# Keeping half of the attention output in SBUF, and another order of the output projection's loads and sums

## The reference

```
mixed = sigmoid(gate_a) * a + sigmoid(gate_h) * r
h  = h + rms_norm(mixed @ w_o, g_mix_post)
hn = rms_norm(h, g_ffn_pre)
ff = (silu(hn @ w_gate) * (hn @ w_up)) @ w_down
h  = h + rms_norm(ff, g_ffn_post)      # meta tokens dropped
```

## Time and profile before

| | |
|---|---|
| median of 3 runs | 2333.02 us (2331.67 to 2337.22) |
| profiled execution, its time | 2335.76 us |
| profiled execution, its span | 2334.0 us |
| mean granted PE clock over the span | 0.98 |
| busy: PE, DVE, ACT, POOL | 2205.8, 1065.7, 917.3, 461.0 us |
| span of the output projection's first matmul to the first FFN tile | 1465.90 to 1580.15 us |

### The profile page before, as it was taken

How to read it: one execution, slowest core, us unless ns; L and a number is a source line. 1 busy time by engine, 2 the same in 40 slices (tenths; PEclk the granted TensorE clock), 3 DMA queues, 4 the chain that set the end, 5 groups by cost and what they waited for, 6 DMA issues and landing times. The chain is left out here.

```text
span 2334.0 us, 32080 instructions
## 1 busy us (share of the span) xinstructions
PE 2205.8 (95%) x11716; PEld 1845.5 (79%) x11716; DVE 1065.7 (46%) x1727; ACT 917.3 (39%) x1454; POOL 461.0 (20%) x213
## 2 busy tenths in 40 slices
PE   5999999999999999889999998789999999999996
PEld 4988888888888888677777776667888788878785
DVE  5003665665764754366666665373533001421102
ACT  4213354354354453544444443444343223222222
POOL 3110000000000000111111111114444444444443
PEclk8999999999999999999999999899999999999998
DMA  3211112111111111211111110542333233343233
GB/s 142 75 63 64 33 60 64 40 59 63 40 59 56 40 57 40 107 41 46 46 45 45 45 45 28 193 145 89 94 132 98 92 108 108 116 136 99 90 104 122
DMA packets 78714, 182.61 MB, mean 78 GB/s; under 512 B 6864, under 2 KB 27664, under 8 KB 78128
## 3 DMA queue, kind: packets, MB, share of 16 engines
q1 hardware_dynamic: 78640, 181.61, 23.9%
HBM read 152.09 MB, written 29.49 MB: 78 GB/s over the span
## 5 line engine op out<-in xcount | busy, mean ns | idle before, releaser
L1798 POOL TENSOR_TENSOR w_lo<-w_raw,w_hi 128x1024 fp32r<-128x1024 f32 x136 | 331.1, 2435 | 398.9 <-ACT w_hi L1807 398.9
L83 PE MATMUL h_bank<-hn_hi,w_hi 128*128 128x512 f32 (+2 forms) x952 | 374.1, 393 | 3.9 <-PEq L165 2.5
L84 PE MATMUL h_bank<-hn_lo,w_hi 128*128 128x512 f32 (+2 forms) x952 | 356.8, 375 | 0.0
L85 PE MATMUL h_bank<-hn_hi,w_lo 128*128 128x512 f32 (+2 forms) x952 | 356.3, 374 | 0.0
L83 PE MATMUL f_bank<-ffn_in_hi,w_hi 128*128 128x512 f32 x768 | 303.5, 395 | 16.7 <-DVE ffn_in_lo L1987 10.9
L85 PE MATMUL f_bank<-ffn_in_hi,w_lo 128*128 128x512 f32 x768 | 301.8, 393 | 0.0
L84 PE MATMUL f_bank<-ffn_in_lo,w_hi 128*128 128x512 f32 x768 | 301.8, 393 | 0.0
L83 PEld LDWEIGHTS h_bank<-hn_hi,w_hi 128*128 128x128 f32 x952 | 179.6, 189 | 36.7 <-issue 9.9
L85 PEld LDWEIGHTS h_bank<-hn_hi,w_lo 128*128 128x128 f32 x952 | 179.4, 188 | 29.8
L84 PEld LDWEIGHTS h_bank<-hn_lo,w_hi 128*128 128x128 f32 x952 | 179.6, 189 | 28.1 <-issue 3.8
L1807 ACT CAST w_hi<-w_raw 128x1024 fp32r<-128x1024 f32 x136 | 142.5, 1048 | 130.7 <-PE f_bank L85 127.9
(11 more groups left out here) (330 smaller groups left out, 4360.5 us busy)
## 6 DMA issues: line engine op xcount, KB each, us to landing
w_raw<-in_w_ffn SPq DMA_DIRECT2D x136, 512.0 KB, 3.6
w_raw<-in_w_hgrn SPq DMA_DIRECT2D x54, 512.0 KB, 3.6
w_raw<-in_w_out SPq DMA_DIRECT2D x15, 512.0 KB, 4.0
w_raw<-in_w_head SPq DMA_DIRECT2D x9, 512.0 KB, 5.7
X<-in_x SPq DMA_DIRECT2D x8, 520.0 KB, 6.5
values<-v_stage SPq DMA_DIRECT2D x32, 128.0 KB, 1.7
values_h<-values SPq DMA_DIRECT2D x8, 512.0 KB, 4.9
gate_out<-raw SPq DMA_DIRECT2D x8, 512.0 KB, 2.9
```

The lines of the kernel that those rows point to most:

```text
L83: pe.matmul(out, wh, xh, start=start, stop=False)
L84: pe.matmul(out, wh, xl, start=False, stop=False)
L85: return pe.matmul(out, wl, xh, start=False, stop=stop)
L1798: pool.tensor_tensor(w_lo[i][:], w_raw[i][:], w_hi[i][:].bitcast(F32), ALU.subtract).then_inc(w_lo_done, 1)
```

## The change

- Attention: the first half of `mixed` is written to `mixed_first`, an SBUF buffer with a place for each head; only the second half goes to DRAM, from one buffer, `mixed_second`. In the last head, after each step j of both segments, ACT casts (`split_high`) and DVE subtracts (`split_low`) one head's first half, eight in all. Their results lie where the latents lay.
- SP no longer waits for the stores at the end of the block; it waits for them in the next one, ahead of the loads of the second half.
- Output projection: the first half needs no loads. Weight loads 1 and 2 go first, then two loads of four second halves each with weight loads 3 and 4 between. They are split after blocks 2 and 4 (`mixed_hi`, `mixed_lo`). The load of x now stands ahead of weight load 6 and waits for all eight.
- `h_inverse_rms(0)` follows block 12 instead of 11, `add_up_h(0)` stands behind k = 6 of block 12 instead of k = 0; the weight casts and normalizing casts of blocks 13 to 15 have another order on ACT, weight subtractions 14 and 15 another on DVE. The first FFN tile waits for each normalized k-tile by itself; `add_up_o(1)` follows it, and all later stages come one tile later. POOL subtracts weight block 16 before it adds the last square.
- `y_sum` gets a buffer of its own, and some buffers lie elsewhere.

```diff
+        self.mixed_first = sb("mixed_first", [P, KT, HALF])
+        with ExitStack() as place:
+            self.mixed_parts = {x: place.enter_context(t.nc.sbuf_tensor(f"mixed_first_{x}", [P, KT, HALF], F32R))
+                                for x in ("hi", "lo")}
...
-        mixed = [sb(f"mixed{i}", [P, HALF]) for i in range(2)]
+
+        def mixed(h, i):
+            return mixed_second[:].unsqueeze(1) if i else lat.mixed_first[:, bass.ds(h.index(), 1), :]
...
-        mixed_out = [signal(f"mixed_out{i}", 16) for i in range(2)]
+        mixed_out = signal("mixed_out", 16)
+        first_hi, first_lo = t.sem("mixed_first_hi"), t.sem("mixed_first_lo")
...
                         sp.dma_start(w_raw[:], dram_block(t.d["w_head"], p.index() + 1)).then_inc(w_in.sem, 16)
                     if h is not None:
-                        for i in range(2):
-                            mix_done.wait(sp, h, i + 1)
-                            sp.dma_start(dram_head(t.d_mixed, hh)[:, i * HALF:(i + 1) * HALF],
-                                         mixed[i][:]).then_inc(mixed_out[i].sem, 16)
+                        mix_done.wait(sp, h, 2)
+                        sp.dma_start(dram_head(t.d_mixed, hh), mixed_second[:]).then_inc(mixed_out.sem, 16)
 
                 iterations(sp, both)
-                for i in range(2):
-                    sp.wait_ge(mixed_out[i].sem, 16 * HEADS)
...
                             gated.wait(pool, x, i + 1)
                             gate_in[i].wait(pool, x, 32)
-                            pool.tensor_tensor(mixed[i][:], mixed[i][:], rec[i][:], ALU.add
+                            pool.tensor_tensor(mixed(x, i), mixed(x, i), rec[i][:].unsqueeze(1), ALU.add
                                                ).then_inc(mix_done.sem, 1)
...
 
+                def split_high(k):
+                    if k == 0:
+                        piece_done.wait(act, At(HEADS - 1), NP_)
+                    mix_done.wait(act, At(k), 1)
+                    act.copy(lat.mixed_parts["hi"][:, k, :], lat.mixed_first[:, k, :]).then_inc(first_hi, 1)
...
                                 values(p)
                             else:
                                 weights(p, 2)
+                        if last:
+                            split_high(which * QS + j)
...
 
+                def split_low(k):
+                    dve.wait_ge(first_hi, k + 1)
+                    dve.tensor_tensor(lat.mixed_parts["lo"][:, k, :], lat.mixed_first[:, k, :],
+                                      lat.mixed_parts["hi"][:, k, :].bitcast(F32), ALU.subtract).then_inc(first_lo, 1)
...
                         if cur is not None and 2 * j + 3 < TILES:
                             low(cur, 2 * j + 3)
+                        if last:
+                            split_low(which * QS + j)
                     if cur is not None:
                         h, i = cur
                         pv_done.wait(dve, h, (i + 1) * TILES)
                         gate_in[i].wait(dve, h, 32)
-                        mixed_out[i].wait(dve, h, 16, lag=1)
-                        dve.tensor_tensor(mixed[i][:], o_bank[:], gate[i][:], ALU.mult).then_inc(gated.sem, 1)
+                        if i:
+                            mixed_out.wait(dve, h, 16, lag=1)
+                        dve.tensor_tensor(mixed(h, i), o_bank[:].unsqueeze(1), gate[i][:].unsqueeze(1), ALU.mult
+                                          ).then_inc(gated.sem, 1)
...
-            ("unused", [P, FT - 2 * KT - 5, HALF], F32), ("normed", [P, 2, HALF], F32), ("f_rs2", [P, HALF], F32))
+            ("out_sum", [P, FT - 2 * KT - 5, HALF], F32), ("normed", [P, 2, HALF], F32), ("f_rs2", [P, HALF], F32))
...
-        mixed = [acts[1], {"hi": mixed_hi2, "lo": mixed_lo2}]
+        mixed = [mixed_first, {"hi": mixed_hi2, "lo": mixed_lo2}]
...
 
-                for i, (half, first, n) in enumerate(MIXED_LOADS):
-                    src = t.d_mixed[first:first + n, :, half * HALF:(half + 1) * HALF].rearrange("k p n -> p k n")
-                    sp.dma_start(mixed_raw[half][:, first:first + n, :], src).then_inc(m_in[i], 16)
-                    if i < 2:
-                        load_out(i + 1)
-                sp.wait_ge(m_hi, 2 * KT)
-                sp.wait_ge(m_lo, 2 * KT)
-                sp.dma_start(x_res, t.d["x"][:, :, 0:HALF]).then_inc(x_in, 16)
-                for b in range(3, OUT_BLOCKS):
+                load_out(1)
+                load_out(2)
+                sp.wait_ge(mixed_out, 16 * HEADS)
+                for i in range(2):
+                    src = t.d_mixed[i * MP_:(i + 1) * MP_].rearrange("k p n -> p k n")
+                    sp.dma_start(mixed_raw[:, i * MP_:(i + 1) * MP_, :], src).then_inc(m_in[i], 16)
+                    load_out(i + 3)
+                for b in range(5, OUT_BLOCKS):
+                    if b == 6:
+                        sp.wait_ge(m_lo, KT)
+                        sp.dma_start(x_res, t.d["x"][:, :, 0:HALF]).then_inc(x_in, 16)
                     if b == OUT_BLOCKS - 2:
...
+                def weight_lo(count, i):
+                    pool.wait_ge(w_hi_done, count)
+                    pool.tensor_tensor(w_lo[i][:], w_raw[i][:], w_hi[i][:].bitcast(F32),
+                                       ALU.subtract).then_inc(w_lo_done, 1)
+
+                for e in range(OUT_BLOCKS - 1):
                     add_square(e)
                 pool.wait_ge(w_lo_done, OUT_BLOCKS - 1)
-                with pool.Fori(0, FFN_BLOCKS) as j:
+                weight_lo(OUT_BLOCKS, 0)
+                add_square(OUT_BLOCKS - 1)
+                weight_lo(OUT_BLOCKS + 1, 1)
+                with pool.Fori(0, FFN_BLOCKS - 1) as j:
                     for i in range(2):
-                        pool.wait_ge(w_hi_done, 2 * j + (OUT_BLOCKS + i))
-                        pool.tensor_tensor(w_lo[i][:], w_raw[i][:], w_hi[i][:].bitcast(F32),
-                                           ALU.subtract).then_inc(w_lo_done, 1)
...
-                def mixed_hi(q):
-                    half, k = q // KT, q % KT
-                    for i, (of_half, first, n) in enumerate(MIXED_LOADS):
-                        if of_half == half and first <= k < first + n:
-                            act.wait_ge(m_in[i], 16)
-                    act.copy(mixed[half]["hi"][:, k, :], mixed_raw[half][:, k, :]).then_inc(m_hi, 1)
+                def mixed_hi(k):
+                    act.wait_ge(m_in[k // MP_], 16)
+                    act.copy(mixed_hi2[:, k, :], mixed_raw[:, k, :]).then_inc(m_hi, 1)
...
 
                 act.preload_act_table_set("natural_log_exp_and_others")
-                for q in range(3):
-                    mixed_hi(q)
                 weight_hi_out(1)
-                for q in range(3, 2 * KT):
-                    mixed_hi(q)
 
                 beside = {0: [lambda m=m: square_h(m) for m in (0, 1)],
                           1: [lambda m=m: square_h(m) for m in (2, 3, 4, 5)],
-                          2: [lambda m=m: square_h(m) for m in (6, 7)], 3: [lambda: h_inverse_rms(0)],
-                          4: [lambda m=m: normed_hi(m) for m in (0, 1, 2)],
-                          5: [lambda m=m: normed_hi(m) for m in (3, 4, 5)],
-                          6: [lambda m=m: normed_hi(m) for m in (6, 7)]}
-                for b in range(OUT_BLOCKS):
-                    if 2 <= b + 1 < OUT_BLOCKS:
+                          2: [lambda m=m: square_h(m) for m in (6, 7)], 4: [lambda: h_inverse_rms(0)]}
+                for b in range(KT + 5):
+                    if b:
                         weight_hi_out(b + 1)
-                    elif b + 1 == OUT_BLOCKS:
-                        act.wait_ge(o_done, b)
-                        weight_hi(2, At(0), 0, 0)
                     if b == KT:
                         o_inverse_rms(0)
                     projected(b)
+                    if b in (2, 4):
+                        for k in range(MP_):
+                            mixed_hi((b - 2) // 2 * MP_ + k)
                     if b >= KT:
                         for step in beside.get(b - KT, []):
                             step()
+                weight_hi_out(KT + 6)
+                normed_hi(0)
+                normed_hi(1)
+                weight_hi_out(KT + 7)
+                normed_hi(2)
+                projected(KT + 5)
+                normed_hi(3)
+                normed_hi(4)
+                projected(KT + 6)
+                act.wait_ge(o_done, KT + 7)
+                weight_hi(2, At(0), 0, 0)
+                for m in range(5, KT):
+                    normed_hi(m)
+                projected(KT + 7)
                 act.wait_ge(h_out, 16)
                 act.wait_ge(o_done, OUT_BLOCKS)
-                tiles(act, 0, feed(0), ("one", lambda: o_inverse_rms(1)), ("over", square_h_step), ("one", nothing),
-                      ("one", lambda: h_inverse_rms(1)), ("over", normed_hi_step))
```

(77 more changed lines are left out.)

20 lines of the change are left out of this document (10 added, 10 removed).

## The result

Over eight runs each, the kernel before takes 2333.03 us (2331.67 to 2337.22) and the kernel after 2345.4 us (2341.67 to 2350.86): ratio 1.0053, 95% interval 1.0041 to 1.0064. It is slower, by 12.4 us between the medians, where -5.3 was forecast.

What follows compares the result with a forecast made beforehand. PE was taken as the bound, so other engines' changes pay only where it waits or runs at low clock. +0.5 up to block 8 and -5.8 around tile 0 gave -5.3 us: 2328 us, range 2321 to 2335.

Steps and rivals of the forecast that it cites:

- The later FFN steps move by one tile, inside slack: 0: FFN stages behind the first tile: each comes one tile later without costing time, 0 us.
- B to E: Rivals in order: load 6 not behind x (0.07); no block 6 stall (0.06); favourable bounds (0.18); last head longer (0.09).
- The last head: Attention's last head: eight added splits lengthen DVE's chain, mostly in the first segment; +2.1 us, bounds 1.3 and 3.5.
- The end of attention and the first projection: SP no longer waits for the last store, -1.7 us; the first projection starts with its block, -8.7 us.
- The 2.0 us for a low clock: Output projection's block 0: takes 5.44 + 2.0 us because PE has idled some 2.9 us; 2.8 for one bound.
- Blocks 1 to 3: Output projection: the stall before block 3 goes, 1.0 us idle comes before block 4; -5.0 us, bounds -6.0 and -4.5.
- Blocks 4 to 7: Output projection: load 6 waits behind x, so PE stalls 11.8 us before block 6, plus 2.0 low clock; +13.8 us.
- Rival B: Output projection: load 6 does not wait behind x; 4.8 us better, 2323 us; chance 0.07.
- rival C: Output projection: no stall at block 6, other work or a looser wait covering it; 13.8 better, 2314 us; chance 0.06.
- Block 13 to tile 1: Block 13's start to the second FFN tile: reordered work shrinks the gaps; -5.8 us, bounds -8.7 and -3.0.
- Before the last head: Attention heads 0 to 6: one store and one DVE wait a head go; 0 us, bounds -0.3 and +0.3.

Runs made afterwards that it cites:

- a_noraw: The kernel after without the added line `of_raw`, 384 unused bytes ahead of the second half's buffers: 2328.85 us, ratio to before 0.9985.
- b_shift384: The kernel before with only 384 unused bytes per partition added ahead of the FFN inputs, no instruction changed: 2350.25 us, ratio to before 1.0075.
- a_xlate: The kernel after with the load of x issued ahead of weight load 9 instead of weight load 6: 2335.08 us, ratio to before 1.0008.

## Why the prediction was wrong

**The step that failed** is "The later FFN steps move by one tile, inside slack: 0", with the "5.44 us" of a block taken as a constant of the machine. The steps do move inside slack; but every matmul of the output block and the FFN was priced as before's, and the k-step went from 681 to 697 ns because the change put operands 384 B off. Measured: +16.6 us from tile 1 to the end, taken away by a_noraw and brought about in the kernel before by b_shift384. No rival had it: B to E dealt with waits, the length of the last head and the clock, none with the pace of the matmuls. The trace of before held the hint, the same k-step at 695 ns in the HGRN stage and 681 in the FFN, both at full clock.

**The last head**, +2.1: the steps are 5.95 us apart instead of 5.35, about 0.60 for each of three, as priced, and from the first to the fourth maximum the head grew by 1.8 (18.11 against 16.35 us). From the fourth to PE's end it took 17.87 us instead of 18.87, so the head as a whole grew by 0.8, under the lower bound of 1.3. The 1.0 was given back by the clock, not by the splits: behind the same 0.55 us idle before ran at a mean granted clock of 0.50 from 1444.20 to 1447.70, and after at 0.83 from 1444.00 to 1447.70. The second multiplication of that step, before and after:

```profile
1445.60 0.63 PE L84 MATMUL a_bank<-prob_lo,v_hi 128*128 128x512 f32 x1
...
1445.33 0.39 PE L84 MATMUL a_bank<-prob_lo,v_hi 128*128 128x512 f32 x1
```

The 0.44 us that the prediction gives as DVE's idle time before each operation of the second segment holds for its last four; the five before them had 0.16 to 1.44.

**The end of attention and the first projection**, -1.7 and -8.7: -12.1. PE idled 2.89 us, as said. The 2.0 us for a low clock did not come in this execution (block 0 took 5.84 us at a mean clock of 1.00); in a_xlate's, with the same 2.89 us ahead, block 0 ran from 1457.31 to 1464.52, 7.21 us at 0.76. So that term varies from one execution to the next: over the seven traces of this schedule block 0 takes 0.3 to 1.8 us more than a block at the full clock, and the 2.8 of the upper bound was not seen.

**Blocks 1 to 3**, -5.0: -4.9, with 0.45 us idle before block 4 instead of 1.0, and 0.16 us more in each block for the pace.

**Blocks 4 to 7**, +13.8: +13.6. The stall was 11.16 against 11.8, the block behind it 7.23 us at a mean clock of 0.76, 1.6 over one at the full clock. Part of the close agreement is chance: the slower pace, which the forecast did not have, adds 0.6 in these four blocks. SP issued x at 1491.41 and PE started at 1503.28, 11.9 us later (12.0 in the earlier trace rows). Rival B is out, since load 6 did wait behind x: x landed at 1499.62 and load 6, issued 0.8 later, at 1500.90, after 8.7 us; rival C is what the kernel becomes when x goes behind load 8.

**Block 13 to tile 1**, -5.8: -4.9. The idle times around tile 0 are 0.76 and 0.83 us and POOL's subtractions release both, as said; before blocks 14 and 15 there are 0.53 and 0.44 that were not, and the pace takes 0.8.

**Before the last head**, 0: after was 2.0 us ahead when it began. It was as far ahead at the first maximum of head 0 (992.14 against 994.16 us), so heads 0 to 6 cost 0.0 in 426 us. A lead ahead of every changed instruction is one execution against another.

Without the placement the forecast would have come near: a_noraw, all of the change but that line, takes 2328.85 us, against 2328.0 forecast and in its range. That it comes within 1 us is luck in part, since terms of 1 to 2 us (the low clock behind a gap, the lead before the last head) differ between executions of one program.

## What to carry to other kernels

Ask of every change what it does to addresses, not only to instructions: one small buffer ahead of the operands of a long matmul stream moved 750 us by 2.2%. When a matmul stream without idle time and at full granted clock has two paces in one trace, compare the places of weights and moving operands; putting the buffers back at multiples of 256 B from each other, by dropping one filler, turned this change's loss of 12 us into a gain of 3 to 4. And a load that moves off one stall has to be followed to the next load queued behind it: the stall moved from block 3 to block 6 and grew, and went only when the load was issued three weight loads later.

## What the runs showed of the hardware

With four fp32r operands in the stream (weights high and low, input high and low), a matmul of 512 columns starts 227 ns after the one before if all of them lie a multiple of 256 B apart, 229 ns if the inputs are 64 B off, and 232 to 233 ns if one or more are 128 or 384 B off (a third of the k-step; single distances are 230 to 236 ns).

Behind a gap of 2.6 or 2.9 us the granted clock fell in some executions of a program and not in others, worth up to 1.8 us each time.

The Trainium skill (SBUF — State Buffer, SBUF: two separate sides) says that within the engine side only the port pair shared by VectorE and GpSimd causes contention, and that PE never waits on anyone; by it b_shift384 would have taken 2333 us, and it took 2350. The Trainium skill (SBUF — State Buffer, A bandwidth-pool intuition that's wrong (but worth ruling out)) gives PE's weight loads a read port of their own; the runs show that the distance between weights and moving operands counts all the same. That the two reads collide in SBUF would fit, but this was argued and not shown: what would tell is a stream with one operand off and no weight load beside it, which was not run.
